# Expert blocks that work on 512 ff columns at a time, with the activations turned on VectorE

## What is computed

```
logits = xt @ w_router
top_val, top_idx = lax.top_k(logits, TOP_K)          # TOP_K = 2
top_w = softmax(top_val)
...
swiglu(xb, w_gate[e], w_up[e], w_down[e])            # for every expert e and its tokens xb
    = (silu(xb @ w_gate) * (xb @ w_up)) @ w_down     # w_gate, w_up: 1024 x 2752; w_down: 2752 x 1024
...
out[token] += top_w * row of its expert
```

## Time and profile before

| | before |
|---|---|
| median of 3 runs | 1289.18 us |
| profiled execution, its own time | 1291.01 us |
| its span, first to last instruction | 1289.1 us |
| granted TensorE clock, mean | 0.996 |
| busy: PE, PEld, DVE, ACT, POOL | 97%, 65%, 46%, 32%, 3% |
| chain that ended last, by engine | PE 77%, DMA 7%, DVE 5% |
| read from HBM | 371.07 MB |

### The profile page before, as it was taken

How to read it: one execution, slowest core, us unless ns; L and a number is a source line. 1 busy time by engine, 2 the same in 40 slices (tenths; PEclk the granted TensorE clock), 3 DMA queues, 4 the chain that set the end, 5 groups by cost and what they waited for, 6 DMA issues and landing times.

```text
span 1289.1 us, 27080 instructions
## 1 busy us (share of the span) xinstructions
PE 1246.2 (97%) x11939; PEld 837.6 (65%) x11939; DVE 592.2 (46%) x1002; ACT 411.7 (32%) x735; POOL 44.0 (3%) x54
## 2 busy tenths in 40 slices
PE   6999999999999999999999999999999999999977
PEld 5787678888887887778755555555555555555533
DVE  6888987654444988988431212012122120211212
ACT  4444563634433544474311211111121111111100
POOL 0011010100000011010000000000000000000010
PEclk9999999999999999999999999999999999999999
DMA  9434434755534344436889999999999999999995
GB/s 345 160 133 162 150 125 153 257 193 196 184 133 149 131 164 146 181 133 254 372 320 400 419 399 389 415 417 419 417 418 419 379 393 422 416 419 417 420 420 237
DMA packets 58062, 376.29 MB, mean 292 GB/s; under 512 B 6322, under 2 KB 6914, under 8 KB 18004
## 3 DMA queue, kind: packets, MB, share of 16 engines
q1 hardware_dynamic: 56866, 370.17, 72.6%
q0 software_dynamic: 1072, 4.33, 1.0%
q10 hardware_dynamic: 2, 0.00, 0.0%
HBM read 371.07 MB, written 3.41 MB: 290 GB/s over the span
## 4 chain that ended last, share of the span: by engine, by line
PE 77%; DMA 7%; DVE 5%; SPq 1%; ACT 1%; issue 1%; POOL 0%; DVEq 0%; ACTq 0%
PE bank L2065 12%; PE bank L1680 8%; PE bank L1681 8%; PE bank L2084 8%; DMA ring<-in_moe 7%; PE bank L2074 6%; PE bank L1981 4%; PE bank L1730 4%; PE bank L2123 4%; PE bank L1958 3%; PE bank L2097 3%; PE bank L2103 3%; PE bank L2114 3%; PE bank L2148 2%; DVE ys L1144 1%; PE bank L2020 1%
## 5 line engine op out<-in xcount | busy, mean ns | idle before, releaser
L1155 DVE TENSOR_TENSOR w_lo<-raw,w_hi 128x2048 fp32r<-128x2048 f32 (+2 forms) x92 | 201.4, 2201 | 52.5 <-ACT w_hi L843 52.3
L1680 PE MATMUL bank<-w_hi,hT_hi 128*128 128x512 f32 (+1 forms) x528 | 209.3, 396 | 2.4 <-DVE hT_lo L1144 1.6
L1681 PE MATMUL bank<-w_hi,hT_lo 128*128 128x512 f32 (+1 forms) x528 | 205.1, 388 | 0.0
L843 ACT ACTIVATE w_hi<-raw 128x2048 fp32r<-128x2048 f32 (+2 forms) x92 | 169.1, 1847 | 88.7 <-PE bank L1730 42.7
L2065 PE MATMUL bank<-ring,hT_block 128*32 128x256 f32 (+1 forms) x2816 | 195.8, 374 | 0.0
L2084 PE MATMUL bank<-ring,hT_block 128*64 128x256 f32 (+1 forms) x1296 | 151.6, 378 | 6.5 <-DMA ring<-in_moe 6.3
L1561 DVE TENSOR_TENSOR both_k<-bank,odd_k 64x256 f32<-64x256 f32 (+1 forms) x44 | 18.1, 410 | 266.9 <-ACT odd_k L1077 266.9
L2065 PEld LDWEIGHTS bank<-ring,hT_block 128*32 128x32 f32 x2816 | 89.7, 110 | 68.6 <-issue 24.8
L1086 ACT ACTIVATE act_T<-bank 128x128 f32<-128x128 f32 (+1 forms) x88 | 26.8, 304 | 332.5 <-PE bank L2148 332.5
L2084 PEld LDWEIGHTS bank<-ring,hT_block 128*64 128x64 f32 x1296 | 88.8, 137 | 67.4 <-issue 17.9
L1565 DVE TENSOR_TENSOR act_moe<-silu_moe,bank 64x256 f32<-64x256 f32 (+1 forms) x88 | 36.7, 417 | 205.0 <-ACT silu_moe L1078 203.6
(11 more groups left out here) (286 smaller groups left out, 1502.3 us busy)
## 6 DMA issues: line engine op xcount, KB each, us to landing
ring<-in_moe SPq DMA_DIRECT2D x232, 1024.0 KB, 16.6
raw<-in_mix SPq DMA_DIRECT2D x56, 1024.0 KB, 4.8
raw<-in_dense SPq DMA_DIRECT2D x30, 1024.0 KB, 4.8
ring<-in_moe SPq DMA_DIRECT2D x16, 768.0 KB, 21.4
ring<-in_moe SPq DMA_DIRECT2D x8, 512.0 KB, 20.5
filters<-in_moe SPq DMA_DIRECT2D x2, 1024.0 KB, 10.1
gate_slots<-in_moe SPq DMA_DIRECT2D x2, 1024.0 KB, 10.8
ring<-in_moe SPq DMA_DIRECT2D x8, 256.0 KB, 18.2
```

Of the source, the lines that this page charges most:

```text
L843: nc.scalar.activation(HI[:, split_slot, 0:width], RAW[:, raw_slot, half:half + width], ACT.Copy)\
L1155: vec.tensor_tensor(LO[:, split_slot, 0:width], RAW[:, raw_slot, half:half + width], HI[:, split_slot, 0:width].bitcast(F32), ALU.subtract ...
L1680: mm(out_, left[0], right[0], start=start, stop=False)
L1681: mm(out_, left[1], right[1], start=False, stop=False)
```

## The change

It touches the expert layer only.

- A chunk is now 512 ff columns (`MOE_CHUNK`), five of them and the last one of 192. The ff columns of a chunk are split into four quarters of 128 (48 in the last), and each quarter goes to its own 32-column tile of PE: tile q computes gate and up, side by side in 256 moving columns, for 32 tokens. A light block has two groups of 32 tokens, a heavy one three, each in a PSUM bank of its own (`gate_up_moe`, `x_banks`). So the result has on partition 32q + i token i of a group, and along it the quarter q of the ff columns.
- ACT applies silu to all groups in one instruction, DVE multiplies in one, and DVE then turns all 32x32 blocks in one instruction (`vec.transpose`), which gives ff rows on partitions in an order that the new weight layout (`moe_slabs`) follows. PE's turns, ACT's copies of them, and the heavy block's odd and even steps are gone.
- A block has 34 slabs: four gate-up slabs and two down slabs a chunk, all of 1 MiB with rows of 8 KB, then two of 768 KB, two down slabs of 1 MiB, one of 512 KB. The last 64 ff rows (256 KB) go as four DMAs of 16 rows by 4 KB into a buffer of their own, `last_rows`, whose other rows are zero. The last down multiplies two full sets of 128 rows.
- The picks for block b + 1 stand in chunk 3 of block b (`PICK_AT`), and write to the second of two token buffers. Block 0 waits for both halves at its start; the others wait in the middle of the block before. ACT and DVE take their copies there too.
- The finished block's rows are stored at slab 14. In the last block DVE adds the gathered rows of both picks of a token half behind chunk 3, and of the other half behind chunk 4 (before: one addition behind each of chunks 6 to 9). POOL clears `last_rows` and `act_last` (the padded activations of the last chunk) before they are used.

The core of the diff:

```diff
+MOE_CHUNK = 2 * CHUNK
+QUARTER = P // 4
+MOE_CHUNKS = FF // MOE_CHUNK
+MOE_SLABS = 34
+PICK_AT = 3
...
+            if p == MOE_SLABS - 1:
+                if at == 0:
+                    sp.wait_ge(sem("last_rows_zeroed"), 1)
+                else:
+                    sp.wait_ge(slab_used, MOE_SLABS * b + first)
+                rows = (TAIL - P) // 4
+                for q in range(4):
+                    sp.dma_start(R["last_rows"][QUARTER * q:QUARTER * q + rows, :],
+                                 slabs["moe"][e, MOE_AT[p] + q * rows * D:MOE_AT[p] + (q + 1) * rows * D]
+                                 .rearrange("o (r n) -> (o r) n", n=D)).then_inc(last_rows_loaded, 16)
+                return
...
-            if p < 4:
-                sp.dma_start(to.rearrange("p (h n) -> p h n", h=2),
-                             slabs["moe"][e, SLAB_AT[p]:SLAB_AT[p + 2]].rearrange("o (h p n) -> p (o h) n", h=2, p=P)).then_inc(loaded, 16)
-                return
...
+                w = quarter(c)
+                nc.scalar.activation(per_group(R["silu_moe"], groups(b), c), x_banks(b, c)[:, :, 0:w], ACT.Silu).then_inc(silu_done, 1)
...
+            def gate_times_up(b, c):
+
+                n, w = groups(b), quarter(c)
+                done_by = (MOE_CHUNKS + 1) * b + (Q_FIRST[1] + c + 1)
...
+                dve.wait_ge(silu_done, done_by)
...
+                vec.tensor_tensor(per_group(act_tile(c), n, c), per_group(R["silu_moe"], n, c), x_banks(b, c)[:, :, w:2 * w], ALU.mult).then_inc(act_done, 1)
+                dve.wait_ge(act_done, done_by)
+                tiles = 4 if c < MOE_CHUNKS else 2
+                vec.transpose(R["act_T"][:, c % 2, 0:tiles, 0:n * QUARTER].rearrange("p j (t c) -> p t j c", t=n),
+                              act_tile(c)[:, 0:n * tiles * QUARTER].rearrange("p (t j f) -> p t j f", t=n, j=tiles)).then_inc(act_turned, 1)
...
+            def gate_up_moe(b, at, k0, nk, c):
+
+                width, tokens = 2 * quarter(c), tokens_of(b)
                 for k in range(nk):
                     kd = k0 + k
+                    for t in range(groups(b)):
+                        for q in range(4):
+                            ins = mm(x_banks(b, c)[QUARTER * q:QUARTER * q + QUARTER, t, 0:width], tokens[:, kd, QUARTER * t:QUARTER * t + QUARTER],
+                                     at[:, (4 * k + q) * width:(4 * k + q + 1) * width], start=kd == 0, stop=kd == KD - 1)
...
+                for c in range(MOE_CHUNKS + 1):
+                    if c == PICK_AT + 1 and isinstance(b, int) and b < NE - 1:
+                        pe.wait_ge(front_ready, b + 2)
+                        pe.wait_ge(rear_ready, b + 2)
+                    slabs_of_c = gate_up_slabs(c)
+                    for i, p in enumerate(slabs_of_c):
+                        nk = KD // len(slabs_of_c)
+                        gate_up_moe(b, loaded(b, p, turns), i * nk, nk, c)
...
+                    pe.wait_ge(act_turned, (MOE_CHUNKS + 1) * b + c)
+                    if c == PICK_AT and isinstance(b, int) and b < NE - 1:
                         pick_tokens(b + 1, ROOM[b + 1])
+                    down_chunk(c - 1)
```

More of the change, by code:

```diff
@@ L109 @@
 SLAB_AT = [P * sum(FFN_WIDTHS[:p]) for p in range(FFN_SLABS)] + [3 * FF * D]
+MOE_WIDTHS = [SLAB] * 28 + [8 * TAIL] * 2 + [SLAB] * 2 + [D, D // 2]
+MOE_AT = [P * sum(MOE_WIDTHS[:p]) for p in range(34)] + [3 * FF * D]
 def raw_value(stage, p):
@@ L159, in freed_by @@
     if b < NE:
[L160 to L163, removed]
+        before, slab = divmod(place_before(place), MOE_PLACES)
+        return before - b, slab
+    place -= MOE_PLACES * b + (2 * RING if p in REJOINED else RING)
+    return (-1, place + MOE_PLACES) if place < 0 else (0, place if place < LATE_SLAB else place - SKIPPED)
 CHUNKS = ["v", "x1", "q", "x2", "k", "av", "g0", "g1", "g2", "g3"]
@@ L704, in slot_free @@
                 blocks, slab = freed_by(at, p)
-                sp.wait_ge(slab_used, FFN_SLABS * b + (FFN_SLABS * blocks + slab + 1 + first))
+                sp.wait_ge(slab_used, MOE_SLABS * b + (MOE_SLABS * blocks + slab + 1 + first))
             elif slot == "h":
@@ L1619, in moe_block @@
                     take_y(b - 1, Y[(b - 1) % 2], free, is_heavy(b - 1)).then_inc(y_taken, 1)
-                for c in range(NCH + 1):
-                    gate_times_up(b, c, heavy)
+                for c in range(MOE_CHUNKS + 1):
+                    gate_times_up(b, c)
+                    if c == PICK_AT and isinstance(b, int) and b < NE - 1:
+                        tokens_rear(b + 1, ROOM[b + 1])
                     if c in between:
@@ L2152, in moe_block @@
[L2152 to L2165 removed]
+                ins = last_third(0)
@@ new lines, in heavy_down, with light_down @@
+                if slabs_done == 2:
+                    ins.then_inc(slab_used, 1)
+                last_third(1)
+                first_two(1).then_inc(slab_used, 1)
+            def light_down(left, rights, start, stop, slabs_done):
+                for k in range(2):
+                    for half in range(2):
+                        ins = mm(Y_BANKS[half][64 * half:64 * half + 64, :], left[:, k, 0:LCAP], rights[k][:, half * 512:half * 512 + 512],
+                                 start=start and k == 0, stop=stop and k == 1)
+                    if k or slabs_done == 2:
+                        ins.then_inc(slab_used, 1)
```

283 lines of the change are left out of this document (115 added, 168 removed).

## The result

The change made the kernel 0.8% slower. Its median is 1299.18 us (1297.86 to 1299.69, 4 runs), beside 1288.85 us before (1288.46 to 1290.49, 4 runs): ratio 1.0079, 95% interval 1.0064 to 1.0094. The forecast was 1281.6 us, and the range, 1275.0 to 1288.5, does not hold it.

What follows compares the result with a forecast made beforehand. The expert weight stream was taken as the bound, except where PE frees slots too slowly. Terms of -6.0, +0.2, -0.8 and -1.0 sum to -7.6 us, giving 1281.6 us on the median; range 1275 to 1288.5.

Steps and rivals of the forecast that it cites:

- Transfers: Expert weight loads: longer rows -1.8 us, four small loads 0, more instruction packets +1.0; together -0.8 us.
- rival A: Expert weight stream: small loads clog it, their 16 rows going to two engines; +35 us in all, 1317 us; 7%.
- Faster PE blocks: Expert blocks: PE saves 3.5 us light, 3.9 heavy, so slots free sooner and lost stream time returns; -6.0 us.
- rival C: Expert stream's slow stretches: all the bytes lost while waiting for PE's pace come back; 1275 us; 18%.
- The stream ends with its slowest engine: End of the expert weight stream: seven more instruction packets cost 0.5 us if shared, 7.5 on one engine; taken as +1.0.
- Picks mid-block: Token picks moved into the block before; only block 0 waits at its start for VectorE's half: +0.2 us.
- The activations: Each expert chunk: silu, product and turn, 0.7 us each, hide behind the next chunk's gate-up; cost 0.
- a sign against me: Expert chunks: the forecast is wrong if PE's waits name VectorE's turn; no size given.
- the rows of 8 KB: First 4 MiB of a block: 8 KB rows replacing 4 KB save 0.3 us a block, -1.8 in seven blocks.
- Behind the last byte: After the last weight load lands: four matmuls of 64x512 remain, 1.9 us where some 3 us followed; -1.0 us.
- The forecast's signs: Expert layer: 415 GB/s or more, no dips near 780 and 1030, heavy PE work under 88 us; wrong if small loads slow it.
- Rules: Small loads: the skill's 2 us per DMA, paid in series, would add 48 us; rows speak against a serial cost.

Runs made afterwards that it cites:

- e2_four_full: Changed kernel with each block's last 256 KB as four loads of 64 KB, each 128 rows of 512 bytes over all partitions: 1285.90 us, ratio 0.9969.
- merged kernel: Changed kernel without its small loads, the last 64 ff rows riding in the 512 KB slab before them, computing everything: 1283.09 us, ratio 0.9956.
- b2_8k_rows: Kernel before the change with rows of 8 KB in each expert's first four slabs: 1288.57 us beside 1289.01, ratio 0.9996.

## Why the prediction was wrong

**The step that failed** is in "Transfers": "Spread over 16 engines they move the same bytes ... I take 0 and keep +3 for the last block". The four loads cost 16.1 us (1299.18 less 1283.09), 2 us a block and not only in the last. I asked whether the bytes were spread over engines, never into which partitions they went. The one row that I had for a 64 KB load ran alone, which shows nothing of how such a load treats a saturated stream, and it is not of this form: `ident` is 128 rows of 512 bytes over all partitions, which is how e2_four_full loads, not 16 rows of 4 KB. So it was no evidence against rival A, and I set it against the whole case. Rival A had the right place, the small loads clogging the stream, with the wrong price, 35 us, the wrong mechanism, two engines, and 7% of the chance; in the kernel after each of the 32 small loads has 16 landings, as a whole slab has, which speaks against two. With the step at +16.1 the sum is 1281.6 + 16.1 = 1297.7, 1.5 us from the result. That is no proof of the rest, as the 16.1 comes from the result itself: it says that the merged kernel (1283.09) lies 1.5 us from the forecast, and the terms below, too small and too large, partly cancel in it, which is luck.

**Faster PE blocks (-6.0).** The direction was right and the size too low. The merged kernel shows it without the loads; its stretches against the earlier trace rows:

```profile
640.00:660.00 20.00, 20.00 (x324) 12.31 (x320) 8.09 (x41) 0.77 (x2) 0.00 (x0) 1.00 0.62 228
660.00:700.00 40.00, 40.00 (x672) 20.78 (x667) 8.27 (x40) 3.02 (x9) 0.00 (x0) 1.00 0.98 391
760.00:800.00 40.00, 37.49 (x664) 23.06 (x660) 4.96 (x10) 2.35 (x5) 0.00 (x0) 0.96 1.01 415
860.00:1000.00 140.00, 137.67 (x2380) 76.80 (x2376) 18.05 (x46) 7.84 (x20) 0.00 (x0) 1.00 1.01 419
1000.00:1060.00 60.00, 58.85 (x949) 37.19 (x940) 8.22 (x21) 3.12 (x7) 0.00 (x0) 1.00 1.01 419
```

By bytes, 40 x 37 / 420 = 3.5 us came back near 780, 60 x 33 / 420 = 4.7 at 1000 to 1060 (I had counted 1.8, by the DMA share), 40 x 10 / 420 = 1.0 up to 700: 9.2 together, counted as rival C counts. The share was a bad guide here: it read 0.98 where 8% of the rate was missing.

**Part of it was given back at the end,** and no step of mine had that. Stretches of the kernel before, then of the merged one:

```profile
1256.00:1268.00 12.00, 10.37 (x88) 5.44 (x88) 1.71 (x2) 0.93 (x3) 0.00 (x0) 1.00 1.01 420
1268.00:1276.00 8.00, 6.33 (x56) 3.56 (x56) 2.20 (x4) 0.98 (x3) 0.00 (x0) 1.00 0.57 232
```

```profile
1240.00:1256.00 16.00, 12.18 (x156) 4.90 (x148) 3.32 (x4) 0.73 (x2) 0.00 (x0) 1.00 0.99 411
1256.00:1268.00 12.00, 9.30 (x156) 4.47 (x158) 4.05 (x7) 0.28 (x2) 0.00 (x0) 1.00 0.49 204
```

The stream doesn't stop at once: some engines are done first, and the others go on at half the rate, 8 us before (a share of 0.57), 12 us in the merged kernel (0.49), some 16 us in the kernel after, from about 1268. Before, (420 - 232) / 420 x 8 = 3.6 us are lost so; in the merged kernel 6.5, with the 0.3 that 411 GB/s cost ahead of it: 2.9 us more. "The stream ends with its slowest engine; I take +1.0" named the effect and was too small. The forecast's seven more instruction packets came (103 for 96), but they are not shown to be the cause.

The trace's landings show how it builds up. From the first of a load's 16 landings to its last it takes 7.6 us near 1000 us in the kernel before, 2.7 near 1040 and 6.5 at the end; in the merged kernel 7.8, 9.3 and 14; in the kernel after 10, 11 and 18. It grows along the stream in all of them, and shrinks clearly only in the kernel before, in the dip of 1000 to 1060 us where the stream waited for PE. So it seems that the dip which the change takes away had let the late parts catch up, and that some of what comes back there is lost at the end. This is read from the traces and was not tried in a run, and what drives the parts apart stays open.

**Picks mid-block (+0.2).** 640 to 660 us moved 228 GB/s in the merged kernel, 219 in the kernel after and 225 before, which is 0.1 us less and 0.3 us more: right, within 0.4 us.

**The activations (0).** I took 0.7 us for each of silu, product and turn. Groups by form after 700 us in the kernel after (busy us, mean ns):

```profile
L1610 DVE STREAM_TRANSPOSE act_T<-act_moe 128x384 f32<-128x384 f32 x20 | 11.6, 578 | 0.7
L1607 DVE TENSOR_TENSOR act_moe<-silu_moe,bank 128x384 f32<-128x384 f32 x20 | 11.1, 555 | 248.4 <-ACT silu_moe L1133 248.4
L1610 DVE STREAM_TRANSPOSE act_T<-act_moe 128x256 f32<-128x256 f32 x15 | 6.7, 445 | 0.5
```

Product and turn are each below 0.7, and so is silu, 491 ns for 128x384. PE's waits in the kernel after do name the turn, which I had given as a sign against me (us in total, times, longest):

```profile
PE bank L2103 <- DMA ring<-in_moe: 22.2, 31, 1.9
PE bank L2134 <- DMA ring<-in_moe: 14.2, 17, 2.1
...
PE bank L2134 <- DVE act_T L1610: 4.2, 3, 1.6
```

Three waits, 4.2 us, all in light blocks (L2134), in a layer where PE waits 36 us for loads anyway; doubling the turn cost at most 0.6 us, so the sign was too strict and the step right.

**Transfers, the rows of 8 KB (-1.8)**: too much; b2_8k_rows found -0.4 (-1.7 to +0.6). **Behind the last byte (-1.0)**: the weights' last landing is at 1269.3 us in the merged kernel and 1276.7 before, and the last half down ends 2.4 and 3.1 us behind it: -0.7, near enough. **The forecast's signs**: the dips near 780 and 1030 went in the merged kernel (415, 419 GB/s), and in the kernel after only in part (401, 401); heavy block 1, which was to take PE under 88 us, took 91.2 with a gap of 3.1 us and 3.4 us at half the clock in it (below); "the rate falls around the small loads" is the sign that came out against the forecast. **Rules**: the 2 us that the Trainium skill (DMA: Bandwidth & Descriptors, Anatomy of one DMA) gives each DMA are fitted there to DMAs that GpSimd issues, and these come from SP. Paid in series they are not to be found here: 24 more loads a run cost 1.4 to 2.2 us in e2_four_full, under 0.1 us each.

Together, for the merged kernel: -9.2 in those stretches, some -1 in the others, +2.9 at the stream's end, about the 7.4 us by which the last landing is earlier, and -0.7 behind it; its profiled span is 7.9 us below that of before (1281.2 for 1289.1). The medians differ by 5.8 to 6.3 us, because the profiled execution of before was 1.8 us above its median.

## What to carry to other kernels

When a stream of loads is the bound, ask of each load into which partitions it goes, not only how many bytes and packets it has: give each one all 128 partitions (every second one did as well here; 16 rows set 8 apart did not), and put an odd remainder into the rows of the load ahead of it. Read a lost stretch by its GB/s, since the DMA share stayed at 1.0 here while the packets took longer. And if a row speaks against a rival's mechanism, ask which other mechanism would give the same symptom before the symptom's chance is set to 7%.

## What the runs showed of the hardware

- One load of 256 KB into 64 neighbouring partitions, once a block, costs a saturated stream 2 us (1299.6 less 1283.7 over 8 blocks); into every second partition 0.1 us (1284.6). The slabs in flight beside it are slowed too (344 and 280 GB/s where 418 is usual), until it has landed.
- In a stream of 1 MiB loads the 16 landings of one load drift apart, by 14 us from first to last at the end of the merged kernel and 18 in the kernel after, and the last 8 to 16 us of the stream run at about half the rate.
- VectorE's turn by 32x32 blocks takes 578 ns for 128x384 and 445 ns for 128x256 floats, near the product of the same size (555 ns).
- In the kernel after the granted clock fell in the expert layer once before the last 3 us, at the end of a gap of 3.1 us in which PE did nothing from 777.6 us on, for a reason that the rows do not show (last columns: clock, share, GB/s):

```profile
775.00:780.00 5.00, 2.64 (x128) 2.43 (x118) 0.00 (x0) 0.00 (x0) 0.00 (x0) 1.00 1.01 416
780.00:785.00 5.00, 4.21 (x31) 2.23 (x34) 0.68 (x2) 0.29 (x1) 0.00 (x0) 0.66 1.02 421
785.00:790.00 5.00, 5.00 (x52) 2.56 (x48) 0.00 (x0) 0.00 (x0) 0.00 (x0) 1.00 1.02 424
```

It was at 1.2 GHz for 3.4 us, from 780.2 to 783.6, and 0.66 in the second stretch is a mean of time at 2.4 and at 1.2 GHz. The stream kept 421 GB/s meanwhile.
